# A hybrid decoder step on one core: order of work around the front stage's convolutions, output reads, decay units and first scores

## The reference

```python
p = _split_in(jnp.einsum('btd,dn->btn', x, w_in))          # one input projection
log_a = jax.nn.log_sigmoid(p['gla_a'] @ w_gla_a2 + b_gla_a) / 16
# mixer A: gated linear attention, 4 heads, chunks of 64
b = jnp.cumsum(log_a, axis=2)                              # in a chunk
q_in, k_in, k_end = q * exp(b), k * exp(-b), k * exp(b_last - b)
att = jnp.where(causal, q_in @ k_in.T, 0)
S = decay * S + k_end.T @ v                                # state, chunk by chunk
o = att @ v + q_in @ S_start
o = o * rsqrt(mean(o * o, -1) + eps) * gla_norm_g * silu(p['gla_r'])
# mixer C: short convolution of width 3 over positions
u = p['conv_c'] * p['conv_h']
y = w[0] * u[t-2] + w[1] * u[t-1] + w[2] * u[t]
o_conv = p['conv_b'] * y
# mixer B: softmax attention with forget terms, then branches, merge, 16 experts
```

## Time and profile before

| what | us |
|---|---|
| runs of the kernel | 1725.12, 1725.51, 1730.22 |
| median | 1725.51 |
| the profiled execution's own time | 1728.11 |
| its span, first to last instruction | 1726.5 |
| TensorE busy in it | 1608.0 |
| VectorE, ScalarE, GpSimd busy | 811.0, 658.0, 240.7 |
| start of the first value unit of the next stage | 423.79 |

### The profile page before, as it was taken

How to read it: one execution, slowest core, us unless ns; L and a number is a source line. 1 busy time by engine, 2 the same in 40 slices (tenths; PEclk the granted TensorE clock), 3 DMA queues, 4 the chain that set the end, 5 groups by cost and what they waited for, 6 DMA issues and landing times. The chain is left out here.

```text
span 1726.5 us, 25621 instructions
## 1 busy us (share of the span) xinstructions
PE 1608.0 (93%) x9847; PEld 1470.6 (85%) x9847; DVE 811.0 (47%) x1295; ACT 658.0 (38%) x1110; POOL 240.7 (14%) x291
## 2 busy tenths in 40 slices
PE   7999989999999999999999999999998499999980
PEld 6988889889998998999999999999787378888860
DVE  4423453354024334322033322223643699999985
ACT  4422151212135455422111211112201288888866
POOL 1000011012001121130000000000000245343320
PEclk8999999999999999999999999999998599999995
DMA  6111133024221112043235124111432789999746
GB/s 170 44 43 37 45 95 90 25 60 132 74 83 52 56 57 78 20 150 107 81 115 177 37 69 145 37 37 53 167 136 76 266 245 276 314 318 269 205 66 228
DMA packets 154225, 204.34 MB, mean 118 GB/s; under 512 B 14724, under 2 KB 121236, under 8 KB 154105
## 3 DMA queue, kind: packets, MB, share of 16 engines
q1 hardware_dynamic: 135224, 140.82, 26.1%
q0 software_dynamic: 18880, 61.89, 12.8%
HBM read 152.34 MB, written 50.34 MB: 117 GB/s over the span
## 5 line engine op out<-in xcount | busy, mean ns | idle before, releaser
L382 PE MATMUL ps<-xh,slab_hi 128*128 128x384 f32 (+1 forms) x504 | 173.9, 345 | 2.4 <-DVE xl L741 2.4
L382 PE MATMUL ps<-xh,slab_lo 128*128 128x384 f32 (+1 forms) x504 | 167.3, 332 | 0.0
L382 PE MATMUL ps<-xl,slab_hi 128*128 128x384 f32 (+1 forms) x504 | 167.1, 332 | 0.0
L1896 PE MATMUL ps<-xh,slab_lo 128*128 128x384 f32 (+1 forms) x384 | 125.2, 326 | 0.0
L1896 PE MATMUL ps<-xh,slab_hi 128*128 128x384 f32 (+1 forms) x384 | 125.1, 326 | 0.0
L1896 PE MATMUL ps<-xl,slab_hi 128*128 128x384 f32 (+1 forms) x384 | 125.1, 326 | 0.0
L2097 DVE TENSOR_TENSOR gt_sg<-ps,gt_sg 128x384 f32<-128x384 f32 (+1 forms) x48 | 25.7, 536 | 186.4 <-PE ps L1896 186.3
L382 PEld LDWEIGHTS ps<-xh,slab_hi 128*128 128x128 f32 x504 | 96.9, 192 | 16.5 <-issue 12.0
L2770 PE MATMUL ps<-mo_hi_gu,mo_xh 128*128 128x512 f32 x256 | 100.3, 397 | 0.9 <-ACT mo_xh L2873 0.7
L2770 PE MATMUL ps<-mo_hi_gu,mo_xl 128*128 128x512 f32 x256 | 98.8, 390 | 0.0
L382 PEld LDWEIGHTS ps<-xl,slab_hi 128*128 128x128 f32 x504 | 96.8, 192 | 0.0
(11 more groups left out here) (466 smaller groups left out, 4209.5 us busy)
## 6 DMA issues: line engine op xcount, KB each, us to landing
slab_raw<-in_w_in SPq DMA_DIRECT2D x60, 512.0 KB, 4.1
mo_raw_g<-in_w_e_gate SPq DMA_DIRECT2D x16, 1024.0 KB, 8.3
mo_raw_u<-in_w_e_up SPq DMA_DIRECT2D x16, 1024.0 KB, 12.9
mo_raw_d<-in_w_e_down SPq DMA_DIRECT2D x16, 1024.0 KB, 6.9
gt_oh<-oT_hi SPq DMA_DIRECT2D x3, 2176.0 KB, 8.1
gt_ol<-oT_lo SPq DMA_DIRECT2D x3, 2176.0 KB, 13.0
slab_raw<-in_w_branch SPq DMA_DIRECT2D x24, 256.0 KB, 4.9
x_dram<-slab_raw SPq DMA_DIRECT2D x9, 512.0 KB, 5.2
```

Source lines behind the costliest of these rows:

```text
L382: mm = eng.matmul(out, w[:, b, k, :], x[:, k, t0:t0 + tn], start=(k == 0 and j == 0), stop=(k == KC - 1 and j == 2), skip_group_check=True)
L1896: last = eng.matmul(out, w[:, s % 2, c, wk, :], x[:, k, t0:t0 + tn], start=(k == 0 and i == 0), stop=(k == ks[-1] and i == 2))
```

## The change

1. TensorE, both pairs: the quarters of slot 0 are issued ahead of the wait for `q_ready` and ahead of the first scores.
2. ScalarE, p = 0: the three decay units are placed ahead of the squares and the copy of the last tile.
3. VectorE, p = 0: the sample states' second update stands inside the convolution of slot 27, behind its second tap. For p = 1 the convolution's last unit is finished in an earlier slot, and the order stays.
4. VectorE, both pairs: the fourth output read (`gate_out(p, 3)`) stands inside the convolution, behind its second tap, ahead of the third.
5. TensorE: the value units' banks go 3, 0, 1, 2 in turn (so do the first key and query units), and each of the first four waits for its own bank alone.

```diff
                 transpose_k(p, 0)
+                fill(p, 0)
                 eng.wait_ge(q_ready, p + 1)
                 for t in range(NT):
                     attend(p, t)
-                    fill(p, 3 * t)
+                    if t:
+                        fill(p, 3 * t)
...
-                copy_out(p, NT - 1)
                 if p == 0:
                     for g in range(3):
                         place(first("a", 1) + g)
+                copy_out(p, NT - 1)
                 copy_state(2 * p)
...
             def convolve(c, between):
...
                     ch(eng.scalar_tensor_tensor(out=y_s, in0=u_s[:, :, j:j + DT], scalar=tap[j], in1=y_s,
                                                 op0=ALU.mult, op1=ALU.add))
+                    if j == 1 and between:
+                        between()
...
-            def serve(p, slot):
+            def serve(p, slot, between=None):
                 for n in finished(p, slot):
-                    place(n)
+                    place(n, between if units[n] == ("h", 2 * p, 2) else None)
...
+                in_taps = ("h", 2 * p, 2) in [units[n] for n in finished(p, 3 * NT)]
                 for b2 in range(4):
-                    carry_sample(p, b2)
-                    serve(p, 3 * NT + b2)
+                    if b2 != 1 or not in_taps:
+                        carry_sample(p, b2)
+                    serve(p, 3 * NT + b2, lambda: carry_sample(p, 1))
...
                 for i in range(6):
-                    gate_out(p, i)
-                    place(first("hb"[i // 3], c) + i % 3) if i < 3 else None
+                    if i != 3:
+                        gate_out(p, i)
+                    place(first("hb"[i // 3], c) + i % 3, lambda: gate_out(p, 3)) if i < 3 else None
...
         def unit_bank(n):
-            return n % 4 if n < kq_unit(1, 0, 0) else 0
+            return (n + 3) % 4 if n < kq_unit(1, 0, 0) else 0
...
                     if n >= 4:
                         eng.wait_ge(unit_free, n - 3)
+                    elif n == 0:
+                        eng.wait_ge(*sh.front.s0_new)
+                        eng.wait_ge(*sh.front.o_out)
+                    else:
+                        eng.wait_ge(*(sh.front.unit_free + [sh.front.bank2])[n - 1])
...
-            for bank in range(2):
-                eng.wait_ge(*sh.front.unit_free[bank])
-            eng.wait_ge(*sh.front.bank2)
-            eng.wait_ge(*sh.front.s0_new)
-            eng.wait_ge(*sh.front.o_out)
```

More of the change, by code:

```diff
@@ L742, in x_tails, with place @@
                                       f32(sh.xh[at]), ALU.subtract).then_inc(x_tail, 1)
-            def place(n):
+            def place(n, between=None):
                 kind, i, g = units[n]
@@ L796, in place @@
                     if g == 2:
-                        convolve(i)
+                        convolve(i, between)
                 elif kind == "b":
@@ L803, in place, with convolve @@
                         tail(b + RH)
-            def convolve(c):
+            def convolve(c, between):
                 for g in range(3):
```

## The result

| | before | changed |
|---|---|---|
| median of nine runs, us | 1725.12 | 1714.11 |
| range of the runs | 1720.46 to 1730.58 | 1713.17 to 1716.51 |
| profiled execution, own time | 1728.11 | 1714.11 |
| its span | 1726.5 | 1712.5 |
| TensorE busy | 1608.0 | 1603.4 |

The ratio of the runs is 0.9936, with a 95% interval of 0.9926 to 0.9946: faster by 11 us between the medians, where 1714.7 us was forecast and 1714.1 came. The two profiled executions lie further apart, 14.0 us.

The account below looks back on a forecast made before the run. TensorE, busy 1608 of 1726.5 us, was taken as the bound; waits of 7.7 us plus 4.4 of clock gave 12.1 us: 1716.0 from the profile, 1713.4 from the median, forecast 1714.7, range 1710.5 to 1719 (eight in ten).

Parts of the forecast that it names:

- given back later: Rival: something behind the front starts at a fixed time, under 5 us is kept, about 1722 us; chance 0.08.
- The piece: Quarters ahead of the first scores cover TensorE's wait for the queries: gain 1.3 us in pair 0, 0.3 in pair 1.
- States: Pair 0's state update between the taps: 1.72 us wait goes, 0.4 stays at the third update; gain 1.3 us.
- Squares: Pair 0's decay units ahead of the squares: the 1.84 us wait falls to 1.0; gain 0.8 us.
- Output reads: Fourth output read between the taps: gain 1.9 us in pair 0, with 0.6 of wait left, and 1.5 in pair 1.
- Value units: First value unit, next stage: using bank 3, it no longer waits for the state copy; gain 1.2 us, nothing late next.
- The store: Pair 1's Abs waits about 0.85 us for the sample states' store, lengthening TensorE's output-read wait; loss 0.6 us.
- The clock: TensorE's 1.2 GHz stretches behind the 1.72, 1.84 and 2.54 us waits all come back; gain 4.4 us together.
- The total: Whole kernel: 12.1 us less, 1716.0 from the profiled execution or 1713.4 from the median; 1714.7 taken, nearly in the middle.
- Only the waits come back: Rival: TensorE's low clock stretches stay or turn up elsewhere, so 7.7 us are saved, 1717.8 us; chance 0.15.
- More than the sum: Rival: no store wait (0.6 us), and the next stage's first-scores low stretch goes too (1.6); 1712.5 us; chance 0.13.
- The store becomes the bound: Rival: the sample states' store lands 17 us after issue, delaying Abs through output read; 1727 us; chance 0.02.

Follow-up runs that it names:

- e4: The kernel before with only the state update and the output reads moved between the convolution's taps; median 1718.20 us, ratio to before 0.9951.
- e5: The kernel before with only the quarters ahead of the first scores and the value units' bank-by-bank waits; median 1722.09 us, ratio to before 0.9977.
- e7: The changed kernel with the quarters ahead of the first scores for pair 0 alone, pair 1 in its old order; 1713.77 us (one run).
- e3: The kernel before with only the decay units placed ahead of the squares; median 1725.51 us, ratio to before 0.9994.
- e6: The changed kernel with pair 0's fourth output read back in its old place behind the convolution; median 1716.06 us, ratio to the kernel before 0.9956.
- e1: The kernel before, unchanged, profiled a second time; 1724.57 us (one run).
- e8: The changed kernel with pair 1's Abs written to the convolution's output buffer, so only the Exp waits for the sample states' store; 1714.40 us, ratio to before 0.9942.
- e10: The same kernel as e8, run and profiled once more; median 1714.79 us, ratio to the kernel before 0.9929.
- e9: As e8, with each wait that the change left worked on by reordering alone; median 1711.62 us, ratio to the kernel before 0.9926.
- e12: As e9, with the third output read ahead of the six instructions bringing decays to the chunk's end; 1711.47 us, ratio to the kernel before 0.9905.
- e13: The kernel before, unchanged, profiled a third time; 1728.62 us (one run).

## Why the prediction was right

*What bounds the kernel.* Right. The time behind the front was 1302.7 us before and 1302.6 after, and it was 1300.7 in e4 and 1303.1 in e5; over all profiles it scatters by 3.7 us without following what the front saves. So the rival "given back later", which would keep under 5 of 12 us, is out; a microsecond given back could not be seen.

*The piece.* Right in place and mechanism, for both pairs: 1.5 and 0.2 us against 1.3 and 0.3. Pair 1's new wait of 0.84 us on line 430 is the one forecast, and e7 shows that without it the trade is nearly even.

*States.* Right: 1.2 us, with a new wait of 0.53 for the third update (0.4).

*Squares.* Right: 0.8 us, 1.01 us of wait left, in e3 alone as in the whole.

*Output reads.* Right: 1.8 us (e6) and 1.7 us (e4), with 0.79 of wait left for the fifth read (0.6).

*Value units.* Right in kind, 1.56 against 1.2 us. Here, as in pair 0's piece and pair 1's read, the gain was 0.2 to 0.3 us above TensorE's idle time. The reason stands in the last two lines of the changed profile above. An idle time is counted from the end of the instruction ahead, but matmuls that follow without a wait overlap in the trace: the value unit starts 0.02 to 0.03 us after the start of the transpose ahead of it, which takes 0.27. Before, it started 1.55 us after that transpose's start, 1.28 of them counted as idle. Going by the distance from start to start, one would have had 1.53. In the same way pair 1's read started 1.87 us after the matmul ahead of it and now starts 0.17 after, a gain of 1.70 where 1.53 was counted.

*The store.* Right: 0.7 us lost against 0.6, with 0.84 us of wait against 0.85. The prediction's own terms (5.1 less 2.9, less 1.45 to spare) make 0.75 us of wait, not 0.85. By the Trainium skill (DMA: Bandwidth & Descriptors, Anatomy of one DMA) the landing was estimated at 2.6 us, which would have given no loss; the trace does not agree, with the second store landing 5.4 us after its issue and 0.84 us of wait.

*The clock.* This is the one step whose reason was wrong. Its size was right for the two executions that were compared, about 4.5 us against 4.4 (1.56, 1.57 and the 1.34 by which e1 is shorter). "The waits that I expect to stay are 0.3 to 1.1 us long, shorter than any that was followed by a fall, so all of it should come back." That all of it did was luck of the draw: in e3, e8 and e10 a stretch followed a wait of 1.0 us, and in e9 and e12 no wait at all. Counted over all profiled executions:

| ahead of the place | profiles | with a stretch behind |
|---|---|---|
| states, wait of 1.7 us | 5 | 4 |
| states, wait of 0.5 us or none | 9 | 0 |
| decay units, wait of 1.8 us | 5 | 5 |
| decay units, wait of 1.0 us | 7 | 3 |
| decay units, no wait | 2 | 2 |
| fourth output read, wait of 2.5 us | 6 | 3 |
| fourth output read, no wait | 8 | 0 |

At two of the three places a fall came only behind the long wait (in 7 of 11 cases, against none of 17 without it), and in some executions only; what decides in which was not tried and stays open. At the third, right behind the decay units (products over 16 rows, 209.8 to 212.1 us in e9), it came with a wait and without one; whether those small products are the reason was not tried. The Trainium skill (TensorE: Matmul & The Clock Gate, Why this matters for your kernels) warns only of longer idle gaps; the trace disagrees, with 7 stretches behind waits of 1.7 to 2.5 us at the two places where none came without a wait.

*The total.* The profiled executions lie 14.0 us apart and the medians 11.0. The profiled execution of before had all three stretches and started up 1.2 us later. A usual one has fewer: by the shares in the table the three are worth 3.5 us and not 4.5, and the changed kernel pays some 0.4 us for those behind its decay units (3 in 7, at the 0.9 us by which D is longer in e8). With 8.2 us of waits, which is 12.67 less the three stretches, this gives 11.3 us, an estimate from few profiles. So the prediction was right to go below its sum of 12.1, for a reason that it gave only as a perhaps; that the middle of its two sums came within 0.6 us of the median is in part luck, for one median of the changed kernel was 1714.1 and the other 1715.2.

*The rivals.* "Only the waits come back" is half true in the decay units' place, where the stretch stayed in e3, e8 and e10. "More than the sum" is out: the store's wait arose, and the stretch at the first scores of the next stage stayed in both profiles of the changed kernel. It was there in two of the three of before (not in e1), so it too comes in some executions only. "The store becomes the bound" is out at a wait of 0.84 to 1.0 us.

## What to carry to other kernels

When a wait is taken away, compute for the next two or three meetings of the same two engines when each would arrive: four of the seven waits here came back shorter, one by one, as computed, and the sum less those was right to 0.6 us. When work is moved forward, look for what it now reaches before something slower is done: here the Abs came forward by more than the store that it must wait for, and 1.5 us to spare became a wait of 0.8. Count what a wait costs from start to start of the instructions around it, not by the idle time. Read a clock stretch from several executions before it is priced; a single profile shows one draw.

## What the runs showed of the hardware

The granted clock of TensorE fell to 0.5 (1.2 GHz) behind the same wait in one execution and not in another: behind the wait of 2.5 us the 24 matmuls took 5.41 us before and 4.44 in e1, at 1.00. Nor was the stretch always of one length: 4.95 us for 18 matmuls in e1, and 5.86 for 19 in e13, where it was twice as long. No such stretch followed the waits of 1.3 to 1.5 us in this stage, in any of the profiles. And it fell with TensorE never idle for more than 0.06 us, behind a run of products over 16 rows: 13.63 us for the 72 matmuls in e9, against 12.1 at full clock.
